# Identity products on TensorE in the head norms of a two-layer hybrid decoder

## The reference, cut to what matters

```
def rms_norm(x, gain):
    xf = x.astype(jnp.float32)
    xf = xf * lax.rsqrt(jnp.mean(xf * xf, axis=-1, keepdims=True) + EPS)
    return (xf * gain.astype(jnp.float32)).astype(x.dtype)
...
    q = rms_norm(q.reshape(B, T, FOX_HEADS, HEAD_DIM), q_norm)
    k = rms_norm(k.reshape(B, T, FOX_HEADS, HEAD_DIM), k_norm)
...
    q = rope(rms_norm(q.reshape(B, T, H, hd), q_norm), pos)
    kc = rope(rms_norm(kv(kc), k_norm[0]), pos)
    ks = rope(rms_norm(kv(ks), k_norm[1]), pos)
    kw = rope(rms_norm(kv(kw), k_norm[2]), pos)
```

## Time and profile before

| | us |
|---|---|
| median of 3 runs | 2351.08 |
| lowest and highest run | 2339.09, 2351.8 |
| profiled execution, whole | 2344.74 |
| its span, first to last instruction | 2342.8 |
| mean granted clock of TensorE in it | 0.924 |
| busy: TensorE, VectorE, ScalarE, GpSimd | 88%, 58%, 34%, 12% |

### The profile page before, as it was taken

The page is one execution under the profiler, slowest core; times in us unless marked ns, Lnnn a source line. Parts: engine busy times, 40 slices in busy tenths (PEclk is TensorE's granted clock), DMA queues, the critical chain, the costliest instruction groups (busy, mean ns, idle before and its releaser), DMA issues. The chain is left out here.

```text
span 2342.8 us, 47717 instructions
## 1 busy us (share of the span) xinstructions
PE 2054.3 (88%) x18117; PEld 1861.6 (79%) x18117; DVE 1351.8 (58%) x2545; ACT 789.6 (34%) x1415; POOL 277.8 (12%) x443
## 2 busy tenths in 40 slices
PE   5986898879999996997799969988987687999998
PEld 3973665659999996995499969988964486999998
DVE  5435432458887634337366558777753358888732
ACT  3111331135454102013266654544421215454300
POOL 0003533000000000000112222212224100000000
PEclk8996988889999997996799989999998998999999
DMA  9347989353333211216410014434359413334221
GB/s 375 98 170 297 345 312 362 121 196 84 99 101 104 93 57 55 75 55 252 155 47 2 2 55 123 121 97 124 109 192 368 171 56 90 106 93 109 96 79 64
DMA packets 239254, 322.56 MB, mean 138 GB/s; under 512 B 18488, under 2 KB 195077, under 8 KB 231724
## 3 DMA queue, kind: packets, MB, share of 16 engines
q1 hardware_dynamic: 215317, 239.18, 31.2%
q0 software_dynamic: 21824, 77.62, 9.6%
q10 hardware_dynamic: 1887, 2.73, 0.3%
HBM read 311.56 MB, written 16.42 MB: 140 GB/s over the span
## 5 line engine op out<-in xcount | busy, mean ns | idle before, releaser
L2663 PE MATMUL ps<-CHi,W1H 128*128 128x256 f32 x768 | 221.7, 289 | 36.5 <-DVE CLo L2766 36.5
L2664 PE MATMUL ps<-CLo,W1H 128*128 128x256 f32 x768 | 219.7, 286 | 0.0
L2665 PE MATMUL ps<-CHi,W1L 128*128 128x256 f32 x768 | 219.5, 286 | 0.0
L959 PE MATMUL ps<-XHup,WLup 128*128 128x272 f32 x640 | 185.1, 289 | 0.0
L959 PE MATMUL ps<-XHup,WHup 128*128 128x272 f32 x640 | 183.8, 287 | 1.3 <-DVE G L1108 1.3
L959 PE MATMUL ps<-XLup,WHup 128*128 128x272 f32 x640 | 184.5, 288 | 0.0
L2663 PEld LDWEIGHTS ps<-CHi,W1H 128*128 128x128 f32 x768 | 149.9, 195 | 38.7 <-DVE CLo L2766 28.3
L2127 ACT ACTIVATE P<-ps,NM 128x128 f32<-128x128 f32 (+1 forms) x224 | 102.1, 459 | 170.5 <-DVE NM L2168 168.9
L486 PE MATMUL ps<-XHdn,WHdn 128*128 128x272 f32 x704 | 147.9, 292 | 12.6 <-remote 5.4
L2664 PEld LDWEIGHTS ps<-CLo,W1H 128*128 128x128 f32 x768 | 150.0, 195 | 0.0
L2665 PEld LDWEIGHTS ps<-CHi,W1L 128*128 128x128 f32 x768 | 149.9, 195 | 0.0
(11 more groups left out here) (572 smaller groups left out, 5343.9 us busy)
## 6 DMA issues: line engine op xcount, KB each, us to landing
H<-in_w_up SPq DMA_DIRECT2D x72, 512.0 KB, 5.0
Wearly<-in_w_mod SPq DMA_DIRECT2D x24, 1024.0 KB, 11.3
RAWdn<-in_w_down SPq DMA_DIRECT2D x14, 1408.0 KB, 6.6
RINGf<-in_cache_fox_k SPq DMA_DIRECT2D x48, 256.0 KB, 6.4
RINGf<-in_cache_fox_v SPq DMA_DIRECT2D x44, 256.0 KB, 7.9
RINGf<-in_cache_fox_v POOLq DMA_DIRECT2D x44, 256.0 KB, 6.1
RAWin<-in_nsa_w_in SPq DMA_DIRECT2D x20, 512.0 KB, 3.6
RINGf<-in_cache_fox_k POOLq DMA_DIRECT2D x38, 256.0 KB, 5.8
```

The lines of the kernel that those rows point to most:

```text
L959: last = self.nc.tensor.matmul(self.ps[:, bank + b, 0:HALF], wt[:, w, k, :], x[:, k, :], start=start and k == 0 and n == 0, stop=k == 3 an ...
L2663: nc.tensor.matmul(out, WH[:, sig, k, w], hi, start=(k == 0 and m == 0), stop=False, skip_group_check=True)
L2664: nc.tensor.matmul(out, WH[:, sig, k, w], lo, start=False, stop=False, skip_group_check=True)
L2665: last = nc.tensor.matmul(out, WL[:, sig, k, w], hi, start=False, stop=(k == KU - 1), skip_group_check=True)
```

## The change

A new function `keep_busy` issues products of the identity by itself, 128 by 128 in fp32, into a PSUM bank that nobody reads. `head_norm` calls it for 8 products ahead of the wait for `b_done` or `added`, for 8 more ahead of the wait for `root`, and for one ahead of each chunk's spread product, behind the wait for `scaled`, into the bank that the spread product then overwrites. With 8 and 14 chunks these are 24 and 30 products. Nothing is removed and nothing else is moved.

```diff
+    def keep_busy(self, bank, count):
+
+        for _ in range(count):
+            self.nc.tensor.matmul(self.ps[:, bank, 0:P], self.ident, self.ident, start=True, stop=True, skip_group_check=True)
@@ head_norm, TensorE
                     pe.wait_ge(early_out, len(early))
+                    self.keep_busy(spread_bank[0] + 1, 8)
                     if rope:
                         pe.wait_ge(b_done, N)
                     else:
                         pe.wait_ge(meal[0]["added"], 1)
+                    self.keep_busy(spread_bank[0] + 1, 8)
                     pe.wait_ge(root, 1)
                     turned_late = 0
                     for t in range(N):
                         if t >= 2:
                             pe.wait_ge(scaled, t - 1)
+                        self.keep_busy(spread_bank[t % 2], 1)
                         j, rr = t // 4, slice(32 * (t % 4), 32 * (t % 4) + 32)
```

## The result

The change makes the kernel slower: 2360.22 us median of 9 runs (2356.33 to 2364.33), against 2348.7 us for the kernel before (9 runs, 2339.01 to 2356.41), 11.5 us between the medians. The ratio of the runs is 1.0063, with a 95% interval of 1.0047 to 1.0079, which is 11 to 18.5 us; the quotient of these two medians alone is 1.0049, and in four later series the kernel before had medians of 2342.87 to 2346.51 us. The prediction was 2349, its range 2337 to 2359, and the likeliest outcome it gave was "same". The case that came true is the rival in which both loops lose their clock, and it cost more than that rival said.

A forecast was written before the change was run, and what follows sets the result against it. It took TensorE, at half clock in both head norm loops, as the bound. First loop holding (-3.8) and second falling (+6.4) gave +2.6 on 2344.74, 2347.3; weighed with the median's 2353.7 it took 2349, range 2337 to 2359.

The forecast's parts named there:

- same: Whole kernel: a measured time not to be told from no change, within about 0.5% or 11.7 us; chance 0.79.
- the rival in which both loops lose their clock: Both head norms' loops fall to half clock: +8.6 us, +11.2 if it never rises ahead of the second; chance 0.30.
- the case that one loop holds its clock: Likelier the first head norm's loop holds, -3.8, and the second's falls, +6.4: +2.6 us, 2347.3; chance 0.45 for either way.
- The price of a filler in the loop: One added identity product ahead of each chunk in both loops: 0.23 us at full clock, 0.43 at half.
- The sum for both falling: Both loops at half clock: +2.2 us from the first head norm and +6.4 from the second, +8.6 together.
- The chance that the clock holds: Full clock to each loop's end: about even for the first, four in ten at most for the second.
- The late starts: First spread product of each loop delayed by identity products ahead: 1.0 us in the first head norm, 3.2 in the second.
- the roots' hole: First head norm, before the loop: TensorE waits 2.71 us for the roots; the second has no such hole to fill.
- the six chunks without turns decide: Opening chunks of both loops, 32-row products plus one identity product each: whether the clock survives them settles the outcome.
- a loop's gain reaches the next stage: A loop holding full clock starts the next stage at full clock: -1.4 us after the first, -1.5 and -0.5 after the second.
- The Trainium skill's rules: Clock falls only for idle TensorE, so both loops hold, 2335.5 us, chance 0.21; transposes don't count as busy.

The follow-up runs named there:

- e7_narrow: The change without the identity products in the waits, and with 16 moving columns instead of 128 in the one ahead of each chunk; one run, 2364.34 us.
- e9_full_rows_and_change: e4_full_rows plus one identity product ahead of each chunk, none in the waits; one run, 2332.65 us.
- e3_first_only: The whole change in the first head norm alone; +4.7 us against the kernel before (0.2 to 9.1).
- e1_waits_only: The change without the identity product ahead of each chunk, the 16 ahead of each loop kept; -1.4 us against the kernel before (-7.3 to +4.5).
- e6_two_then_none: The change with two identity products ahead of each of chunks 0 to 5 and none later; +4.0 us against the kernel before (-1.2 to +9.4).
- e4_full_rows: The kernel before with spread products on all 128 rows, weights zero-padded, no identity products; -9.9 us, ratio 0.9958 (0.9940 to 0.9976).
- e5_full_rows_hole: e4_full_rows plus nine identity products in the hole ahead of the first loop; -15.2 us against the kernel before, -11.0 us when run again.
- e11_loads_first: e5_full_rows_hole with the two modulation weight loads issued ahead of the window-state copies; -12.0 us against the kernel before (-16.0 to -7.7).

## Why the prediction was wrong, point by point

The forecast rested on the case that one loop holds its clock, +2.6 us. Neither did, which is the rival of +8.6, and that rival was 2.8 us too small (11.4 in the profile). The first error made the middle of the forecast wrong, the second carried the time over the end of its range.

- **The price of a filler in the loop**: this is the step that failed, in the chunks without turns. The sum put it at 0.23 us at full clock, in a chain through VectorE of 0.97 us a chunk, and at 0.43 at half. It is 0.6 us and 1.0, TensorE becomes the bound, and these chunks take 1.11 and 1.93 us, where 0.97 and 1.29 were forecast. The rows taken for the price were of products among their like. The kernel before held the sign: of a chunk with turns, 0.49 of 2.25 us were "switching", for two changes between the kinds. A filler between spread products adds two such changes, and the prediction gave it none. e7_narrow and e9_full_rows_and_change show it. With turns the price at half clock was right (2.67 against 2.25 + 0.43 = 2.68), because there the filler stands behind transposes, and adds no change that wasn't there.
- **The sum for both falling**: +2.2 and +6.4 us, measured +3.1 and +8.3. The difference lies almost wholly in the six chunks without turns: 6.74 us in the first loop where the kernel before had 5.74, and 8.02 where it had 6.03. So they cost +1.0 and +2.0 us, where the sums leave about +0.3 and -0.2 for them. The eight chunks with turns of the second loop cost +3.4, as forecast. By its sum from the median the range ended at 2359, and 2360.22 is what it took.
- **The chance that the clock holds**: given as even for the first loop and four in ten for the second. It fell in both, and in e3_first_only too. The argument was that a filler in each chunk feeds the clock; e1_waits_only shows that the clock lasted as long without it, and e6_two_then_none that it took two. All nine runs of the changed kernel are at 2356.33 or above, and eight of nine before at or below 2351.8, so it is unlikely that this was settled anew in each run; only one run was profiled, so it isn't shown. The prediction read the scatter of the runs before as a sign that it might be; e1_waits_only (2330.91 to 2359.06) has more scatter still, from a cause that isn't known.
- **The late starts**: forecast 1.0 and 3.2 us, measured 1.2 and 2.9. The price of a filler among its like, 0.23, was 0.235. The clock rose 3.5 us after TensorE's restart at 1091.4, where 4 was taken.
- **What was right**: that the roots' hole exists in the first head norm alone; that the six chunks without turns decide, since with two identity products in each the clock held on through the turns. That a loop's gain reaches the next stage holds for the first head norm, whose eight small transposes step by 0.11 us in e4_full_rows instead of 0.21. It fails for the second in e4_full_rows and e5_full_rows_hole, where TensorE waits for weights and restarts at half clock (8 products in 1.94 us), and in e6_two_then_none, where the clock falls in the break; e11_loads_first has it. The transfer that then comes due wasn't in the sum.
- **The Trainium skill's rules**: the page "TensorE: Matmul & The Clock Gate" of the Trainium skill has the clock fall for idle time (section on HAM oscillation). Here it fell while TensorE was busy 4.00 of 4.00 us. Part 4 of the same page of the Trainium skill has transposes not count as busy in the same way. In e6_two_then_none transposes with 32-row products, and nothing else, kept the clock at 1.00 for 10.6 us.

## What to carry to other kernels

Work that is put in only to hold TensorE's clock has to be priced beside its neighbours, at the place where it goes: among products on other rows of the array it costs two changes of kind, and a place in a loop it costs every time. Here it was cheaper to make the needed product bigger in rows than to add one: the same columns on 128 rows, padded with zero weights, brought the clock back within the loops, held it in the first head norm once the hole ahead was filled, and removed the changes of kind as well. And when a stretch gets shorter, look which transfer was covered by it.

## What the runs showed of the hardware that was not expected

- Changing between 32-row and 128-row products costs TensorE about 0.2 us each way at full clock and 0.3 at half (1.11 against 0.50 + 0.22 us a chunk, and 1.93 against 0.91 + 0.42, for two changes). With all products on 128 rows it wasn't seen (1.17 us with an identity product against 0.95 without).
- TensorE can be busy all the time and still lose its clock: 32-row products with one identity product for each four fell to 0.50 after 5.6, 3.8 and 3.0 us, with two they held 1.00 for the 7.3 us that they lasted.
- 32-row products and transposes held 1.00 for 10.6 us (e6_two_then_none) but stayed at 0.50 for 17.1 us (the kernel before): in these two profiles the mixture kept whichever level it met.
- Making the same spread products use all 128 rows, three quarters of them with zero weights, brought the clock from 0.50 to 1.00 in 3.4 us (e4_full_rows).
